# Two fused transformer blocks on one core: where the modulation pieces stand in the projection tiles, which engine copies the compressed probabilities, and when the top-k rounds run

## The chip, the cores and the metric

One NeuronCore of a Trainium2 chip runs the whole kernel. The metric is the device time of one execution in microseconds. TensorE (PE) multiplies, ScalarE (ACT) applies functions, VectorE (DVE) and GpSimd (POOL) do elementwise work and reductions, and SyncE (SP) issues the transfers (DMA) from memory into the on-chip buffers.

## The reference

Two blocks follow each other on x (1 x 512 x 1024, float32). The first is modulated by a vector c, has two attention groups and a feed-forward part; the second has two feed-forward parts with a stick-breaking attention and a recurrent group between them. The change touches only the first block up to its attention, which is, cut to what matters:

```
mod = c @ w_ada + b_ada                       # 6 x 1024 numbers: sh1, sc1, gt1, sh2, sc2, gt2
h = rms_norm(x, g_pre_mix) * (1 + sc1) + sh1
proj = h @ w_in                               # queries, keys, values, index queries and keys, gates
o_nsa = gates x (compressed + selected + window attention)     # 8 heads, 2 key groups
o_dsa = attention over the 128 keys of highest index score     # 8 heads, 1 key group
x = x + gt1 * rms_norm(concat(o_nsa, o_dsa) @ w_out, g_post_mix)
```

The compressed branch has 32 keys (one is padding), made by a small two-layer network from the rotated keys and values. The index score of a query and a key is a weighted sum of four rectified products; the top 128 of a row of up to 512 scores are found by 16 rounds of "find the 8 largest, then replace them" for each of the query tiles 1, 2 and 3 (48 rounds).

## The kernel before, in words

Activations lie with features on the 128 partitions and the 512 tokens along the free axis. Each weight tile of 128 output features is split into a high and a low part (ScalarE writes the high one, L913; VectorE the rest, L1280), and a product is three matmuls (L342 to L344). The weight tiles come in one fixed order (`STREAM`) through four ring slots.

All engines run a program written out in order, and wait on semaphores. The change lies between 58 us and 335 us of the span:

- **Projection tiles 0 to 15** (loop `for n in range(16)` on TensorE). A tile is 8 steps of k with three matmuls each, 24 matmuls. Tile 0 to 8 (`WIDE = 9`) run as a whole. ScalarE copies each finished tile (`projected`, L991), which releases `ropein`; four SP transfers swap its halves (`turn_halves`, L1882), and VectorE rotates it (`rope`).
- **The late modulation.** The last four of the six modulation vectors need 16 pieces of `w_ada` of 1 MB each (`ada_late`). They pass through two buffers: piece i goes into buffer i % 2. TensorE multiplies one with `late_piece(i)` (L404). In tiles 0 to 3 and 5 to 8 two pieces stand behind the tile's 24 matmuls; tile 4 has the step `ada_cols(1)` there (L413) instead. `logits` (L443) of the index scores follow from tile 3 on, `compress(0)` (L453) behind tile 7.
- **SP's order.** SP loads a piece with `late_load(i)` (L1856), which waits until the piece two before has been used. Pieces 2n+2 and 2n+3 (for n = 0 to 3, and one less in number for 5 to 7) stand in SP's program behind `turn_halves(n)`, which waits for `ropein` of tile n, and behind the weight tiles of `after[n]`. SP issues in order.
- **The mixed stage, tiles 9 to 15.** After every second k, TensorE runs one `pair_step(p)`, p = 0 to 27; steps 28 to 50 follow without a tile. Step p makes the scores of head pair p (L478), turns the probabilities of pair p-2 (`turn_probs`, L494) and multiplies those of pair p-3 with the values (`pv`, L510). The widths follow a pattern: query tile 3 (512 keys), 0 (128), 2 (384), 1 (256). VectorE masks the scores and takes their minimum (`masked`, L1447), ScalarE exponentiates (L1021), VectorE and POOL scale, and ScalarE copies the turned probabilities out of the bank (L1008, L1002).
- **The compressed branch** runs four times in it, at the steps of `CMP_AT`: scores at step p, softmax on VectorE at p and p+1 (`cmp_masked`, L1479; `cmp_probs`, L1492 to L1498) with one exponential on ScalarE (L1025), the turning at p+2 (`cmp_turn`, L529), the copy of the turned probabilities out of bank 4 in the same step (VectorE, L1516), and the product at p+4. `cmp_keys` prepares its 32 keys at step 4. TensorE cannot turn pair p-2 into bank 4 before this copy is done.
- **Top-k rounds** (`top_round`, L1394 and L1395) are put on VectorE at the end of tiles 5 to 8 (2 each) and then of the pair steps (one each, two in every fourth step), and end at step 31. Step 32 uses the last mask.

Of the kernel before, what the change touches and what calls it, by code (L numbers as in the profile page):

```python
# [12 lines left out]
ACT = mybir.ActivationFunctionType  # L13
# [5 lines left out]
KD = D // P  # L19
# [9 lines left out]
ROUNDS = TOPK // 8  # L29
# [107 lines left out]
def build(nc, xt, consts, cols, pos, ada, ada_late, mats, extra, out):  # L137
    ctx = ExitStack()
    with ctx:
        sems = {}  # L140

        def S(name):
            if name not in sems:
                sems[name] = ctx.enter_context(nc.semaphore(name))
            return sems[name]
# [138 lines left out]
        NP = len(pairs)  # L284
# [7 lines left out]
        steps = [(hh, c) for hh in range(HEADS) for c in (3, 2, 1, 0)]  # L292
        SLOTS = 14
        WIDE = 9
        CMP_AT = [7, 10, 18, 26]
        OUT_AT = [12, 19, 27, 35, 39, 43, 47, NP]
        slot_steps = [list(range(3 * n, min(3 * n + 3, 32))) for n in range(SLOTS)]

        NORMS = ["pre1", "post1", "f1", "post2", "g1", "mix", "g2"]
# [11 lines left out]
        def _(pe):  # L311
# [105 lines left out]
            def late_piece(i):  # L417

                q, k = i // KD, i % KD
                pe.wait_ge(S(f"ada_in{i % 4}"), 16 * (i // 4 + 3))  # L420
                if k == 0:
                    claim(7, "ada_rows", q + 2)
                ada_sums(k, ada_late_in[i % 2], range(4)).then_inc(S("ada_sums"), 1)
# [117 lines left out]
            def pair_step(p):  # L541

                if p < NP:
                    qk(p)
                if p == 0:
                    ada_cols(2)
                    compress(1)
                if p == 4:
                    cmp_keys()
                if p in CMP_AT:  # L550
                    if p == CMP_AT[0]:
                        pe.wait_ge(S("cmp_kv"), 1)
                    cmp_scores(CMP_AT.index(p))
                if p - 2 in CMP_AT:
                    cmp_turn(CMP_AT.index(p - 2))
                if p - 4 in CMP_AT:
                    cmp_out(CMP_AT.index(p - 4))
                if 2 <= p < NP + 2:
                    turn_probs(p - 2)
                if 3 <= p:  # L560
                    pv(p - 3)

            for n in range(16):
                b = n % 2 if n < WIDE else 0
                claim(b, "ropein", n + 1)
                w = take("w_in", P, "proj_full", n + 1)
                for k in range(KD):
                    mm = product(bank[:, b, :], [v[:, k, :] for v in w], [hs[:, part, k, :] for part in (0, 1)],
                                 k == 0, k == KD - 1)
                    if k == KD - 1:  # L570
                        mm.then_inc(S("proj_full"), 1)
                    if n >= WIDE and k % 2 == 1:
                        pair_step(4 * (n - WIDE) + k // 2)
                if n < 4:
                    late_piece(2 * n)
                    late_piece(2 * n + 1)
                elif n == 4:
                    ada_cols(1)
                elif n < WIDE:
                    late_piece(2 * n - 2)  # L580
                    late_piece(2 * n - 1)
                if 3 <= n < WIDE:
                    logits(2 * (n - 3))
                    logits(2 * (n - 3) + 1)
                if n == 7:
                    compress(0)
# [301 lines left out]
        def _(act):  # L888
# [120 lines left out]
                           .then_inc(S("probT"), 1)  # L1009

            def outputs(n):
                act.wait_ge(S("pv"), 9 if n == 0 else LAST_PAIR[n] + 1)
                act.activation(out_at(0, n), bank[:, 6 + (n + 1) % 2, :], ACT.Copy).then_inc(S("oT_hi"), 1)

            def pair_step(p):
                t, br, i = pairs[p]
                kv = (t + 1) * P
                for e in range(2):
                    n = 2 * (p % 2) + e
                    act.wait_ge(S("smin"), 2 * p + e + 1)  # L1020
                    act.activation(soft[p % 4][:, e, 0:kv], soft[p % 4][:, e, 0:kv], ACT.Exp, scale=-1.0,  # L1021
                                   bias=smin[:, n:n + 1], accum_out=ssum[:, n:n + 1]).then_inc(S("probs"), 1)
                if p in CMP_AT:
                    act.wait_ge(S("cmp_shift"), CMP_AT.index(p) + 1)
                    act.activation(cs[:, 1, :, :], cs[:, 0, :, :], ACT.Exp, scale=-1.0).then_inc(S("cmp_exp"), 1)  # L1025
                    own("cmp_exp")
                if p >= 2:
                    probs_turned(p - 2)
                if p == 2:
                    act.wait_ge(S("cmp_hid"), 2)  # L1030
                    act.activation(hidc[:, :, :, :].rearrange("p m g n -> p (m g n)"), bank[:, 6, 0:4 * CMP_N],
                                   ACT.Gelu_apprx_tanh).then_inc(S("cmp_gelu"), 1)
                    log_exp_tables()
                if p in OUT_AT:
                    outputs(OUT_AT.index(p))

# [217 lines left out]
        def _(dve):  # L1254
# [149 lines left out]
            for n in range(WIDE):  # L1404
                if n >= 1:
                    rope(n - 1)
                if n == 5:
                    mod_cols(1)
                ahead("w_in", n, ("w_in", 15))
                if 3 <= n:  # L1410
                    index_score(2 * (n - 3))
                    index_score(2 * (n - 3) + 1)
                while n >= 5 and rounds < 2 * (n - 4):
                    top_round(rounds)
                    rounds += 1

# [85 lines left out]
            for p in range(NP + 1):  # L1502
                if p < NP:
                    masked(p, 0)
                    masked(p, 1)
                    if p == 0:
                        late_mods()
                    if p == 4:
                        cmp_keys()
                    if p in CMP_AT:  # L1510
                        cmp_masked(CMP_AT.index(p))
                    if p - 1 in CMP_AT:
                        cmp_probs(CMP_AT.index(p - 1))
                    if p - 2 in CMP_AT:
                        dve.wait_ge(S("cmp_turned"), CMP_AT.index(p - 2) + 1)
                        dve.tensor_copy(cpt.rearrange("p a b -> p (a b)"), bank[:, 4, 0:256]).then_inc(S("cmp_probT"), 1)  # L1516
                        own("cmp_probT")
                if p >= 1:
                    scaled(p - 1)
                if p in OUT_AT[:-1]:  # L1520
                    outputs(OUT_AT.index(p))
                if p % 4 == 1 and p // 4 + WIDE < 16:
                    lo(PINDEX["w_in", min(p // 4 + WIDE + 2, 15)])
                if p == 41:
                    lo(PINDEX["w_out", 2])

                while p < NP and rounds < min(3 * ROUNDS, 2 * (WIDE - 5) + 5 * (p + 1) // 4):
                    top_round(rounds)
                    rounds += 1
            outputs(2 * NT - 1)  # L1530
# [467 lines left out]
```

## Time and profile before

| what | value |
|---|---|
| median of 3 runs | 2175.61 us (2174.71 to 2176.11) |
| profiled execution | 2178.61 us, of it 2176.8 us span |
| TensorE busy | 1993.5 us, 92% of the span |
| VectorE busy | 929.9 us, 43% |
| ScalarE busy | 701.8 us, 32% |
| GpSimd busy | 201.3 us, 9% |
| mean granted TensorE clock | 0.958 |
| read from memory | 168.36 MB, 78 GB/s over the span |

The shares are means over stages with different limits. TensorE is nearly full over most of the span; the stretch that the change touches is the one where it waits most. The time of a kernel here is the time of TensorE's program: each wait of TensorE lengthens it, and nothing behind 385 us depends on the other engines' lead in this stretch. A profile row of a timeline has the start, the time it took, and in square brackets the idle time ahead of it and what ended that.

### The profile page before, as it was taken

To read this page: it belongs to the slowest core of one execution; us is meant where nothing else is said; L and a number is where in the kernel's file an instruction comes from. 1 tells how busy PE (TensorE), PEld (TensorE's weight loads), DVE (VectorE), ACT (ScalarE), POOL (GpSimd) and SP (SyncE) were. 2 spreads that over 40 slices of the span, in tenths; PEclk is the share of its full clock that TensorE was granted. 3 is DMA by queue.
4 is the path that set the end of the run, shared out by engine and by line. 5 is a ranking of instruction groups with operands and counts; after the bars stand their busy time and mean duration, and the time that the engine had idled before them with its cause. 6 is when DMAs were issued, how large, how long until landed. Compare 5 with 4: busy or idle time off the path is not lost. (4 is left out here: it accounts for less than half of the span.)

```text
span 2176.8 us, 25083 instructions
## 1 busy us (share of the span) xinstructions
PE 1993.5 (92%) x10172; PEld 1535.8 (71%) x10172; DVE 929.9 (43%) x1534; ACT 701.8 (32%) x1139; POOL 201.3 (9%) x165
## 2 busy tenths in 40 slices
PE   5888977889999999999999889995888899999999
PEld 3555654768888876888888666653777767888887
DVE  4245776363434435332332423347434354332332
ACT  3224446242322333221222445562111143221231
POOL 0012434200000010000002003340000010000000
PEclk9898999989999999999999999997989999999999
DMA  8652100212222221232232111100000022332231
GB/s 346 236 208 72 30 25 30 78 49 97 97 96 90 96 97 52 97 113 77 97 122 72 68 68 39 39 20 0 1 1 1 1 87 78 101 112 78 97 113 52
DMA packets 44467, 176.02 MB, mean 81 GB/s; under 512 B 5568, under 2 KB 5824, under 8 KB 41024
## 3 DMA queue, kind: packets, MB, share of 16 engines
q1 hardware_dynamic: 44352, 174.41, 23.4%
q8 instruction: 81, 1.33, 0.3%
q14 instruction: 34, 0.28, 0.0%
HBM read 168.36 MB, written 2.10 MB: 78 GB/s over the span
## 5 line engine op out<-in xcount | busy, mean ns | idle before, releaser
L342 PE MATMUL bank<-hs,wsp 128*128 128x512 f32 x1368 | 550.3, 402 | 22.5 <-DVE hs L1319 11.5
L913 ACT ACTIVATE wsp<-ring 128x1024 fp32r<-128x1024 f32 (+2 forms) x244 | 268.7, 1104 | 854.7 <-PE bank L344 852.1
L343 PE MATMUL bank<-hs,wsp 128*128 128x512 f32 x1368 | 539.6, 394 | 0.0
L344 PE MATMUL bank<-hs,wsp 128*128 128x512 f32 x1368 | 538.8, 394 | 0.0
L1280 DVE TENSOR_TENSOR wsp<-ring,wsp 128x1024 fp32r<-128x1024 f32 (+2 forms) x244 | 311.9, 1281 | 410.9 <-ACT wsp L913 410.8
L342 PEld LDWEIGHTS bank<-hs,wsp 128*128 128x128 f32 x1368 | 261.2, 191 | 100.1 <-issue 38.8
L344 PEld LDWEIGHTS bank<-hs,wsp 128*128 128x128 f32 x1368 | 260.9, 191 | 56.1
L343 PEld LDWEIGHTS bank<-hs,wsp 128*128 128x128 f32 x1368 | 261.6, 191 | 54.5 <-issue 1.9
L344 PE MATMUL bank<-hids,wsp 128*128 128x512 f32 x608 | 241.0, 396 | 0.0
L343 PE MATMUL bank<-hids,wsp 128*128 128x512 f32 x608 | 241.0, 396 | 0.0
L342 PE MATMUL bank<-hids,wsp 128*128 128x512 f32 x608 | 241.0, 396 | 0.0
L1790 POOL TENSOR_TENSOR arena<-arena 128x512 f32<-128x512 f32 x24 | 43.3, 1802 | 1102.6 <-ACT arena L925 1102.6
L343 PEld LDWEIGHTS bank<-hids,wsp 128*128 128x128 f32 x608 | 114.5, 188 | 27.9
L344 PEld LDWEIGHTS bank<-hids,wsp 128*128 128x128 f32 x608 | 114.5, 188 | 27.9
L342 PEld LDWEIGHTS bank<-hids,wsp 128*128 128x128 f32 x608 | 114.5, 188 | 27.9
L1588 DVE SCALAR_TENSOR_TENSOR x<-bank,x 128x512 f32<-128x512 f32 x40 | 27.7, 691 | 173.6 <-PE bank L344 173.6
L1578 DVE TENSOR_TENSOR tmp<-tmp,bank 128x512 f32<-128x512 f32 x44 | 30.2, 687 | 128.5 <-PE bank L344 128.5
L1021 ACT ACTIVATE arena<-arena,smin 128x512 f32<-128x512 f32 (+3 forms) x96 | 53.1, 554 | 88.9 <-DVE smin L1447 88.9
L494 PE MATMUL bank<-cst,arena 128*128 128x128 f32 x240 | 41.1, 304 | 29.4 <-DVE arena L1516 11.7
L404 PE MATMUL bank<-arena,c 128*32 128x512 f32 x176 | 28.6, 751 | 38.0 <-DMA arena<-ada_late 21.6
L1225 ACT ACTIVATE wal<-bank 128x512 f32<-128x512 f32 x40 | 23.9, 597 | 116.8 <-PE bank L794 116.8
L494 PEld LDWEIGHTS bank<-cst,arena 128*128 128x128 f32 x240 | 27.7, 151 | 47.6 <-ACT tmp L1008 13.7
(290 smaller groups left out, 2198.8 us busy)
## 6 DMA issues: line engine op xcount, KB each, us to landing
ring<-m_gate SPq DMA_DIRECT2D x44, 512.0 KB, 3.3
ring<-m_up SPq DMA_DIRECT2D x44, 512.0 KB, 3.2
ring<-m_down SPq DMA_DIRECT2D x32, 704.0 KB, 4.0
ring<-m_w_in SPq DMA_DIRECT2D x38, 512.0 KB, 3.3
arena<-ada_late SPq DMA_DIRECT2D x16, 1024.0 KB, 8.0
ring<-m_w_up SPq DMA_DIRECT2D x32, 512.0 KB, 3.3
ring<-m_w_down SPq DMA_DIRECT2D x32, 512.0 KB, 3.2
ring<-m_w_out SPq DMA_DIRECT2D x16, 512.0 KB, 3.5
```

The source lines that it names most:

```text
L342: pe.matmul(out, lhs[0], rhs[0], start=start, stop=False)
L343: pe.matmul(out, lhs[0], rhs[1], start=False, stop=False)
L344: return pe.matmul(out, lhs[1], rhs[0], start=False, stop=stop)
L404: mm = pe.matmul(bank[32 * j:32 * j + 32, 7, :], c32[:, k, :], tile[:, n * T:(n + 1) * T], start=(k == 0), stop=(k == KD - 1), skip_group_ ...
L494: mm = pe.transpose(bank[:, b, (c + k) * P:(c + k + 1) * P], soft[p % 4][:, e, k * P:(k + 1) * P], const("ident"))
L913: act.activation(wsp[:, s % SPLIT, 0, 0:size], ring[:, i % RING, 0:size], ACT.Copy)\
L1021: act.activation(soft[p % 4][:, e, 0:kv], soft[p % 4][:, e, 0:kv], ACT.Exp, scale=-1.0, bias=smin[:, n:n + 1], accum_out=ssum[:, n:n + 1]) ...
L1225: act.activation(PP[:, (lv + 1) % 2, 1, :], bank[:, 6, :], ACT.Copy).then_inc(S("powerT"), 1)
L1280: dve.tensor_tensor(wsp[:, s % SPLIT, 1, 0:size], ring[:, i % RING, 0:size], wsp[:, s % SPLIT, 0, 0:size].bitcast(F32), ALU.subtract).then ...
L1578: dve.tensor_tensor(f, f, bank[:, 2 * (nn % 2) + 1, :], ALU.mult).then_inc(S("gated"), 1)
L1588: dve.scalar_tensor_tensor(out=x[:, nn, :], in0=bank[:, nn % 4, :], scalar=scale, in1=x[:, nn, :], op0=ALU.mult, op1=ALU.add).then_inc(S(" ...
L1790: pool.tensor_tensor(sq[:, 0, :], sq[:, 0, :], sq[:, k, :], ALU.add).then_inc(S("sq_sum"), 1)
```

## The change

Five edits. In tiles 0 to 3 and 5 to 8 the first of the two modulation pieces moves from the tile's end behind k = 3, the second stays at the end. `CMP_AT` becomes 9, 12, 18, 26 (it was 7, 10, 18, 26), `OUT_AT[0]` 14, and `cmp_keys` stands at step 6. The copy of the turned compressed probabilities goes from VectorE to ScalarE, there behind the two exponentials of its step. The top-k rounds are four in each of tiles 5 to 8 (16 by the end of tile 8, they were 8), and then one in every pair step up to 31.

```diff
-        CMP_AT = [7, 10, 18, 26]
-        OUT_AT = [12, 19, 27, 35, 39, 43, 47, NP]
+        CMP_AT = [9, 12, 18, 26]
+        OUT_AT = [14, 19, 27, 35, 39, 43, 47, NP]
...
-                if p == 4:
+                if p == 6:
                     cmp_keys()
...
-                if n < 4:
-                    late_piece(2 * n)
-                    late_piece(2 * n + 1)
-                elif n == 4:
-                    ada_cols(1)
-                elif n < WIDE:
-                    late_piece(2 * n - 2)
-                    late_piece(2 * n - 1)
+                    if n == 4 and k == KD - 1:
+                        ada_cols(1)
+                    elif n < WIDE and n != 4 and k in (3, KD - 1):
+                        late_piece(2 * (n - (n > 4)) + k // 4)
...
-                act.wait_ge(S("pv"), 9 if n == 0 else LAST_PAIR[n] + 1)
+                act.wait_ge(S("pv"), 11 if n == 0 else LAST_PAIR[n] + 1)
...
+                if p - 2 in CMP_AT:
+                    act.wait_ge(S("cmp_turned"), CMP_AT.index(p - 2) + 1)
+                    act.activation(cpt.rearrange("p a b -> p (a b)"), bank[:, 4, 0:256], ACT.Copy)\
+                       .then_inc(S("cmp_probT"), 1)
...
-                while n >= 5 and rounds < 2 * (n - 4):
+                while n >= 5 and rounds < 4 * (n - 4):
...
-                    if p - 2 in CMP_AT:
-                        dve.wait_ge(S("cmp_turned"), CMP_AT.index(p - 2) + 1)
-                        dve.tensor_copy(cpt.rearrange("p a b -> p (a b)"), bank[:, 4, 0:256]).then_inc(S("cmp_probT"), 1)
-                        own("cmp_probT")
...
-                while p < NP and rounds < min(3 * ROUNDS, 2 * (WIDE - 5) + 5 * (p + 1) // 4):
+                while p < NP and rounds < min(3 * ROUNDS, ROUNDS + p + 1):
```

TensorE's order before, at the end of tile 1 (`ada_in2` and `ada_in3` are the loads of pieces 2 and 3):

```order
L344 MATMUL bank<-hs,wsp 128x512
L404 MATMUL bank<-arena,c_77 32x512 [waits ada_in2]
L404 MATMUL bank<-arena,c_77 32x512 x3
L404 MATMUL bank<-arena,c_77 32x512 [waits ada_in3]
L404 MATMUL bank<-arena,c_77 32x512 x3
L342 MATMUL bank<-hs,wsp 128x512 [waits w_lo,ropein]
```

TensorE's order now, in the middle of tile 1:

```order
L344 MATMUL bank<-hs,wsp 128x512
L404 MATMUL bank<-arena,c_77 32x512 [waits ada_in2]
L404 MATMUL bank<-arena,c_77 32x512 x3
L342 MATMUL bank<-hs,wsp 128x512
L343 MATMUL bank<-hs,wsp 128x512
```

The wait for piece 2 now has twelve matmuls of the same tile in front of it and twelve behind it. SP's order between tiles 0 and 2 is the same before and after; the first transfer of each `tmp<-tmp` group waits for ScalarE's copy of the finished tile:

```order
L1882 DMA tmp<-tmp 32x512 [waits ropein]
L1882 DMA tmp<-tmp 32x512 x3
L1862 DMA ring<-m_w_in 128x1024 [waits w_lo]
L1856 DMA arena<-ada_late 128x2048 [waits ada_sums] x2
L1882 DMA tmp<-tmp 32x512 [waits ropein]
```

So the loads of pieces 2 and 3 stay behind the end of tile 0. VectorE's order before, from the second round of step 19 to step 20:

```order
L1394 MAX best_65<-arena 128x8
L1395 MATCH_REPLACE arena<-best_65,arena 128x512
L1447 ISA arena,smin<-bank,cst 128x512
L1447 ISA smin 128x1
L1447 ISA arena,smin<-bank,cst 128x512
L1447 ISA smin 128x1
L1516 COPY arena<-bank 128x256
L1457 RECIPROCAL rsum<-ssum 128x2
```

VectorE's order now at the same place (one round in step 19, no copy in step 20):

```order
L1469 TENSOR_TENSOR oalt<-bank,oalt 128x512
L1394 MAX best_65<-arena 128x8
L1395 MATCH_REPLACE arena<-best_65,arena 128x512
L1447 ISA arena,smin<-bank,cst 128x512
L1447 ISA smin 128x1
L1447 ISA arena,smin<-bank,cst 128x512
L1447 ISA smin 128x1
L1457 RECIPROCAL rsum<-ssum 128x2
```

ScalarE's order now, at the turn to a step that has the copy (L1017 are the exponentials, which wait for VectorE's minimum; L1025 is the copy):

```order
L1017 ACTIVATE arena,ssum<-arena,smin 128x256 [waits smin]
L998 ACTIVATE arena<-bank 128x2x128 [waits probs_turned,pv]
L1009 ACTIVATE oalt<-bank 128x512 [waits pv]
L1017 ACTIVATE arena,ssum<-arena,smin 128x512 [waits smin] x2
L1025 ACTIVATE arena<-bank 128x256 [waits cmp_turned]
L1004 ACTIVATE tmp<-bank 128x384 [waits probs_turned,pv]
```

The copy has moved from behind VectorE's two masks to behind ScalarE's two exponentials, which themselves follow those masks.

## Rows read from the trace of the kernel before

**Rows 1.** Busy us by engine (PE, PEld, DVE, ACT, POOL), granted clock, DMA share, GB/s
```profile
103.00:170.40 67.40, 55.87 (x279) 35.90 (x277) 26.81 (x49) 12.79 (x21) 11.52 (x9) 0.85 0.57 212
```

**Rows 2.** Timeline of TensorE, 60 to 170 us: start, time, instructions [idle before <-releaser]
```profile
63.87 1.92 PE L404 MATMUL bank<-arena,c 128*32 128x512 f32 x16
...
75.11 1.65 PE L404 MATMUL bank<-arena,c 128*32 128x512 f32 x8 [3.62 <-DMA arena<-ada_late]
79.30 1.93 PE L404 MATMUL bank<-arena,c 128*32 128x512 f32 x8 [2.53 <-DMA arena<-ada_late]
...
87.33 1.92 PE L404 MATMUL bank<-arena,c 128*32 128x512 f32 x16
...
96.78 1.07 PE L404 MATMUL bank<-arena,c 128*32 128x512 f32 x8 [1.82 <-DMA arena<-ada_late]
100.00 1.93 PE L404 MATMUL bank<-arena,c 128*32 128x512 f32 x8 [2.15 <-DMA arena<-ada_late]
...
143.96 7.36 PE L453 MATMUL bank<-arena,ring 128*128 128x64 f32 x64
...
162.79 1.93 PE L404 MATMUL bank<-arena,c 128*32 128x512 f32 x8 [5.93 <-DMA arena<-ada_late]
...
170.39 0.78 PE L342 MATMUL bank<-hs,wsp 128*128 128x512 f32 x1
```

**Rows 3.** Waits of TensorE, 60 to 520 us: us in total, times, longest
```profile
PE bank L404 <- DMA arena<-ada_late: 21.6, 8, 5.9
...
PE bank L494 <- DVE arena L1516: 11.7, 3, 5.5
```

**Rows 4.** Timeline of SP's issues behind tiles 0, 2 and 7: start, time, transfer
```profile
64.95 2.48 SPq L1882 DMA_DIRECT2D tmp<-tmp  x4
...
68.10 0.93 SPq L1856 DMA_DIRECT2D arena<-ada_late  x2
...
91.14 0.93 SPq L1856 DMA_DIRECT2D arena<-ada_late  x2
...
153.15 1.51 SPq L1856 DMA_DIRECT2D arena<-ada_late  x2
```

**Rows 5.** Timeline of TensorE in the mixed stage, steps 20, 28 and 33
```profile
279.70 1.05 PE L494 MATMUL bank<-cst,arena 128*128 128x128 f32 x6 [4.26 <-DVE arena L1516]
...
318.56 1.54 PE L494 MATMUL bank<-cst,arena 128*128 128x128 f32 x6 [5.47 <-DVE arena L1516]
...
334.08 0.48 PE L478 MATMUL bank<-arena 64*128 64x128 f32 x2 [1.61 <-DVE smin L1447]
```

**Rows 6.** Timelines of VectorE (steps 27 and 28) and of ScalarE (last row)
```profile
315.34 0.69 DVE L1394 MAX8 best<-arena 128x8 f32<-128x512 f32 x1
...
316.86 0.69 DVE L1447 CUSTOM_DVE_ANT_0 arena<-bank,cst 128x512 f32<-128x512 f32 x1
...
318.08 0.42 DVE L1516 COPY arena<-bank 128x256 f32<-128x256 f32 x1
```
```profile
318.31 0.70 ACT L1021 ACTIVATE arena<-arena,smin 128x512 f32<-128x512 f32 x1
```

**Rows 7.** Timeline of TensorE: 1st and 13th matmul of tiles 1, 2, 4; also the 8th of tile 4
```profile
65.72 0.50 PE L342 MATMUL bank<-hs,wsp 128*128 128x512 f32 x1
...
68.62 0.39 PE L342 MATMUL bank<-hs,wsp 128*128 128x512 f32 x1
...
81.16 0.80 PE L342 MATMUL bank<-hs,wsp 128*128 128x512 f32 x1
...
84.52 0.39 PE L342 MATMUL bank<-hs,wsp 128*128 128x512 f32 x1
...
103.01 0.79 PE L342 MATMUL bank<-hs,wsp 128*128 128x512 f32 x1
...
106.17 0.41 PE L343 MATMUL bank<-hs,wsp 128*128 128x512 f32 x1
...
107.33 0.39 PE L342 MATMUL bank<-hs,wsp 128*128 128x512 f32 x1
```

More of the change, by code:

```diff
@@ L1507, in _ @@
                         late_mods()
-                    if p == 4:
+                    if p == 6:
                         cmp_keys()
```

## The prediction

> **What bounds the kernel now.** I read the timeline of TensorE first, because it is busy over 92% of the span and its program is one fixed order. From 103 to 170 us it is busy for 55.9 of 67.4 us, at a granted clock of 0.85 [rows 1]. The waits there end with the landing of a modulation piece: 3.62 and 2.53 us in tile 1, 1.82 and 2.15 in tile 3, 5.93 in tile 8 [rows 2], 21.6 us in eight waits in all [rows 3]; tile 6 has a pair like tile 3's. Tile 2 has none: its two pieces run at once [rows 2], since they were issued while TensorE waited in tile 1. So one tile in two waits.
>
> SP's timeline tells why a piece is late. The load of the next two pieces stands behind the four transfers that turn the finished tile, and these begin when ScalarE has copied it: tile 0 ends at 63.9, the turning begins at 64.95, the pieces are issued at 68.10 [rows 4], 4.2 us behind the tile's end. Behind tile 2 it is 91.14 - 87.33 = 3.8. From issue to use is 75.11 - 68.10 = 7.0 us in tile 1, 96.78 - 91.14 = 5.6 in tile 3, 162.79 - 153.15 = 9.6 in tile 8 [rows 2, 4]. The second piece of a pair is there 4.2 and 3.2 us behind the first [rows 2].
>
> In the mixed stage TensorE waits for VectorE's copy of the compressed probabilities, 4.26 us at step 20 and 5.47 at step 28 [rows 5]. Such waits take 11.7 us in all [rows 3], the third is one of 2.0 us; a fourth step waits 0.3 for VectorE. The copy itself takes 0.42 us; it is late because VectorE did two top-k rounds and two masks ahead of it [rows 6].
>
> **The pieces (the large term).** The multiplication of a piece is the same work in either place, 0.96 us at the full clock (16 records in 1.92). What counts is what stands between a piece's issue and its use. Before, behind tile n: the rest of the pieces, tile n+1 whole, then the wait. Now: the second piece of tile n, half of tile n+1, then the wait, and the other half of tile n+1 behind it. SP's order is the same, and piece 2n+2 cannot be issued before tile n has ended and been copied. An earlier use of the buffer brings no earlier load. The wait begins about half a tile earlier, and the half tile behind it has lost its cover. It also now delays the end of tile n+1, with it the copy, SP's turning and the issue of the next pair. Every tile waits, where one in two did.
>
> From the end of one such tile to the end of the next is then a chain: 3.8 us to the issue, the landing, one piece, half a tile. One piece behind a wait takes 1.93 us in three rows of five, 1.65 and 1.07 in the others; I take 1.9. Half a tile takes 68.62 - 65.72 = 2.9 us without a wait, 84.52 - 81.16 = 3.4 when it follows a wait and a piece directly (tile 2), 107.33 - 103.01 = 4.3 when logits stand between (tile 4) [rows 7]. Tile 4's first seven matmuls took 106.17 - 103.01 = 3.16 us at the low clock, 0.45 each; twelve would take 5.4. I take 4.3: in tile 4 most of the slow stretch was already spent on the logits, and the waits now are longer.
>
> | end of tile | chain | at |
> |---|---|---|
> | 0 | 63.9 + one piece 0.95 | 64.9 |
> | 1 | + 4.2 + 7.0 + 1.9 + 4.3 | 82.3 |
> | 2 | + 3.8 + 6.3 + 1.9 + 4.3 | 98.6 |
> | 3 | + 3.8 + 5.6 + 1.9 + 4.3 | 114.2 |
> | 5 | + piece 0.9, logits 1.2, tile 5.6, columns and logits 1.6, tile 5.6, piece 0.9 | 130.0 |
> | 6 | + 3.8 + 6.3 + 1.9 + 4.3 | 146.3 |
> | 7 | + the same 16.3 | 162.6 |
> | 8 | + piece 0.9, logits 1.1, compress 7.2 (7.36 in its row, the end overlaps) [rows 2], then 2.0 + 9.6 + 1.9 + 4.3 | 189.6 |
> | start of tile 9 | + piece 0.9, logits 1.1 | 191.6 |
>
> The 6.3 is the mean of 7.0 and 5.6. Tile 5 doesn't wait, since its pieces are issued behind tile 3 and tile 4 stands between: issued at 118.0, landed by about 124.4, wanted at 126.2. Tile 8 costs little more than before: the loads of the compress weights hold its pieces for 9.6 us in either order, and before, the whole tile and the wait took as long. Before, tile 9 starts at 170.4 [rows 2], with about 0.5 us still to lose to the slow clock. The term is 191.6 - 170.4 - 0.5 = **+20.7 us**.
>
> Its bounds, from the rows: five chains of 3.8 + 5.6 + 1.1 + 3.4 = 13.9 us instead of 81.9 in all give 12 less, **+9**; five of 4.2 + 7.0 + 1.9 + 5.4 = 18.5 give 11 more, **+32**.
>
> The slow half tile is the term that I know least. The Trainium skill ("TensorE: Matmul & The Clock Gate", "HAM oscillation — how this bites in real kernels") describes just this loop: short stretches of matmuls between waits for loads, each of which starts at the low clock, so that the price of a change of clock is paid once per stretch. The pieces behind the waits at 79.30, 100.00 and 162.79 agree, at 1.93 us for 0.96 us of work. By that rule taken to its end every half tile runs at the low clock, which is a rival below. A second page speaks for shorter chains: by "DMA: Bandwidth & Descriptors" of the same Trainium skill ("Anatomy of one DMA — SWDGE (gpsimd) path", given for GpSimd's path), a transfer costs about 2.0 us plus its bytes at 436 GB/s, an estimate of 4.4 us for 1 MB. The five chains would be 9 us shorter by it. No load of a piece landed that soon in this trace, and other loads stand ahead of each in the queue, so I stay with the rows.
>
> **More top-k rounds in tiles 5 to 8.** Eight more rounds of about 0.98 us (256 wide) on VectorE, four per tile instead of two. They lie in tiles where TensorE waits for loads; tiles 6, 7 and 8 leave VectorE over 8 us idle each. Behind tile 8 VectorE has then 3.9 us of rounds ahead of the first mask instead of 2; TensorE meanwhile runs the logits, the first scores and 7.3 us of compress, and asks for that mask's bank only at the second pair. Cost nothing; without that cover 2 us.
>
> **Fewer rounds in the mixed stage.** Steps 19, 27 and 31 lose one 512-wide round each, 316.86 - 315.34 = 1.5 us [rows 6], just where VectorE is last.
>
> **The copy on ScalarE.** VectorE copied at 318.08, right behind its second mask. ScalarE has the same mask to wait for, then the second exponential (it began at 318.31 and took 0.70) and the reading of its sum, 0.19: it could begin at 319.2, 1.1 us later, for a copy of equal length. That is +1.1 at each of the four places while TensorE waits there. With the lost round: step 20, -1.6 + 1.1 = -0.5; step 28, -1.5 + 1.1 = -0.4. The first two now lie at steps 11 and 14. Step 11 had at its old place 0.3 us of wait, and VectorE does two masks, the compressed softmax (1.8), a weight tile (1.2) and two rounds in the steps ahead: I take +1.0. Step 14 likewise has one round less but a weight tile more: +0.4.
>
> **The other shifts.** `cmp_keys` at step 6 waits for the same 10 small copies on VectorE as at step 4 (a wait of 2.25 us before): 0. The compressed scores at step 9 and 12 wait less for VectorE than at 7 and 10 (0.53 and 1.62 us before), -1.0. At step 33 the wait of 1.61 us for the mask [rows 5] goes, since step 31 has one round less: -1.5; ScalarE's copies are late next there.
>
> **The sum.** Mixed stage: 1.0 + 0.4 - 0.5 - 0.4 - 1.0 - 1.5 = -2.0, between -6 (the copy's lateness hidden, and less slow clock behind each wait) and +4 (the copy late in full at all four, no gain from the rounds). Total +20.7 - 2.0 = **+18.7 us**. The profiled execution of 2178.6 would become 2197.3; the median of the runs is 3.0 below the profiled one, so 2175.6 + 18.7 = **2194.3 us**.
>
> **Rivals.**
> - *Half clock throughout.* TensorE is idle some 6 us in each 16 and never gets its clock back within a half tile: chains of 18.5 us, +32 - 2 = +30, 2205.6. For it: 1.93 us for a piece behind each longer wait. Against: tile 2 was back at full pace within three microseconds of its wait [rows 7].
> - *VectorE was the real limit (faster).* If the mixed stage's waits are all VectorE's lateness, the 8 rounds and four copies taken off it remove the 11.7 us of waits for L1516, 1.6 at step 33, and about 6 us of slow clock behind them: -19. With the projection at its low bound, +9, it ends 10 us faster, 2165.6. It decides from the point at which ScalarE's copy is done when TensorE has turned the compressed probabilities; [rows 6] speak against it, since the masks and exponentials ahead alone take over 2 us.
> - *The change doesn't do what it says to the waits.* SP could have the pieces loaded ahead of the turning, and the earlier use of a buffer would count. Then the 21.6 us of waits for pieces [rows 3] would go, -20, 2155. The issues behind the turning [rows 4] and SP's order nearly exclude it.
> - *Small sum.* Chains at the low bound and the mixed stage at its best, with ends near +4: 2179.6. It needs every term at its low end.
>
> **How the numbers follow.** Forecast 0.75; half clock 0.13; small sum 0.06, half of it within 0.2% (4.4 us, about what a measurement of this kernel can tell from no change) and half above; VectorE the limit 0.04; earlier loads 0.02. Slower 0.91, same 0.03, faster 0.06. The range goes from +7 (the term's low bound less 2) to +30, 2182 to 2206.
>
> **What the profile after would show.** In each of tiles 1, 2, 3, 6, 7 and 8 one wait of 5 to 9 us for `ada_late` behind the 12th matmul, none or little at the tile's end, none in tile 5; SP's issues of pieces 3.8 us behind each tile's end; tile 9 starting near 191. In the mixed stage waits of about 3.8 and 5.1 us at steps 20 and 28, now for ScalarE. It would be wrong if the tiles follow each other at less than 14 us, which a landing in 5 us or a clock that stays high would do, or if the mixed stage is shorter by more than 6 us.

## The result and the profile after

The changed kernel takes 2191.9 us (median of 6 runs, 2182.1 to 2198.8) against 2175.4 us before (6 runs). The ratio is 1.0075, 95% interval 1.0056 to 1.0093: slower by 16.3 us, between 12 and 20. Forecast were 18.7 us and 2194.3 us. The profiled execution took 2185.3 us (span 2183.5) and lies in the faster half of its runs; its granted clock, told below, goes with that.

The piece waits moved into the tiles and grew. This is TensorE's timeline after, the rows of the pieces alone, to set beside [rows 2]. The pieces without a bracket stand at a tile's end and find their data there:

```profile
66.39 1.07 PE L404 MATMUL bank<-arena,c 128*32 128x512 f32 x8
76.57 1.94 PE L404 MATMUL bank<-arena,c 128*32 128x512 f32 x8 [6.16 <-DMA arena<-ada_late]
82.46 1.07 PE L404 MATMUL bank<-arena,c 128*32 128x512 f32 x8
91.89 1.94 PE L404 MATMUL bank<-arena,c 128*32 128x512 f32 x8 [5.40 <-DMA arena<-ada_late]
98.57 1.07 PE L404 MATMUL bank<-arena,c 128*32 128x512 f32 x8
108.11 1.93 PE L404 MATMUL bank<-arena,c 128*32 128x512 f32 x8 [5.48 <-DMA arena<-ada_late]
113.61 1.07 PE L404 MATMUL bank<-arena,c 128*32 128x512 f32 x8
...
128.41 1.90 PE L404 MATMUL bank<-arena,c 128*32 128x512 f32 x8 [3.03 <-DVE mod L1290]
133.96 1.06 PE L404 MATMUL bank<-arena,c 128*32 128x512 f32 x8
...
143.88 1.93 PE L404 MATMUL bank<-arena,c 128*32 128x512 f32 x8 [5.06 <-DMA arena<-ada_late]
150.20 1.07 PE L404 MATMUL bank<-arena,c 128*32 128x512 f32 x8
...
159.64 1.94 PE L404 MATMUL bank<-arena,c 128*32 128x512 f32 x8 [4.59 <-DMA arena<-ada_late]
164.97 1.07 PE L404 MATMUL bank<-arena,c 128*32 128x512 f32 x8
...
185.76 1.94 PE L404 MATMUL bank<-arena,c 128*32 128x512 f32 x8 [8.55 <-DMA arena<-ada_late]
191.66 1.06 PE L404 MATMUL bank<-arena,c 128*32 128x512 f32 x8
```

There is one wait in the middle of every tile that has pieces, none at its end, and each piece behind a wait takes nearly twice the time of the one without (1.94 and 1.07 us).

SP's timeline after, to set beside [rows 4], has the issue 3.8 us behind the tile's end (86.27 - 82.46, and 102.39 - 98.57), as before:

```profile
83.19 2.41 SPq L1878 DMA_DIRECT2D tmp<-tmp  x4
85.64 0.58 SPq L1858 DMA_DIRECT2D ring<-m_w_in  x1
86.27 0.93 SPq L1852 DMA_DIRECT2D arena<-ada_late  x2
...
102.39 0.93 SPq L1852 DMA_DIRECT2D arena<-ada_late  x2
```

TensorE's largest waits from 60 to 520 us after, to set beside [rows 3]:

```profile
PE bank L404 <- DMA arena<-ada_late: 35.2, 6, 8.6
PE bank L494 <- ACT arena L1025: 10.7, 3, 4.8
```

The waits for pieces grew from 21.6 to 35.2 us; those for the compressed copy are 10.7 where they were 11.7, and end now with ScalarE's copy (L1025). At step 20 and 28, to set beside [rows 5]:

```profile
295.23 1.08 PE L494 MATMUL bank<-cst,arena 128*128 128x128 f32 x6 [3.50 <-ACT arena L1025]
...
333.18 1.54 PE L494 MATMUL bank<-cst,arena 128*128 128x128 f32 x6 [4.82 <-ACT arena L1025]
```

For all kernels below, three marks divide the span: the first score product (step 0, L478), the first product with `w_out`, and the end. Between the first two lies the mixed stage. "Idle" is what TensorE's busy time leaves of it, so it holds all its waits, and "clock" is the mean granted TensorE clock in it. All numbers are of the profiled execution.

| kernel | step 0 at | w_out at | mixed stage | idle in it | clock in it | rest | span |
|---|---|---|---|---|---|---|---|
| before | 172.3 | 385.4 | 213.1 | 34.9 | 0.93 | 1791.4 | 2176.8 |
| after | 195.3 | 395.2 | 199.9 | 29.6 | 0.97 | 1788.3 | 2183.5 |
| pieces only (e1) | 198.0 | 406.9 | 208.9 | 34.9 | 0.95 | 1788.9 | 2195.8 |
| all but pieces (e2) | 172.2 | 379.5 | 207.3 | 29.6 | 0.93 | 1793.5 | 2173.0 |
| loads first (e3) | 157.4 | 363.3 | 205.9 | 30.7 | 0.94 | 1788.7 | 2152.0 |
| piece behind k = 5 (e4) | 181.4 | 390.3 | 208.9 | 29.6 | 0.93 | 1787.9 | 2178.2 |
| pieces at end, loads first (e5) | 153.7 | 363.5 | 209.8 | 30.0 | 0.92 | 1790.0 | 2153.5 |
| copy only (e6) | 173.6 | 387.3 | 213.7 | 37.0 | 0.93 | 1788.9 | 2176.2 |
| rounds only (e7) | 176.1 | 382.5 | 206.4 | 29.4 | 0.93 | 1786.2 | 2168.7 |
| shift only (e8) | 174.8 | 382.2 | 207.4 | 34.1 | 0.95 | 1788.4 | 2170.6 |
| columns early (e14) | 190.5 | 401.0 | 210.5 | 28.1 | 0.90 | 1790.3 | 2191.3 |
| loads first, columns early (e11) | 153.5 | 360.9 | 207.4 | 30.7 | 0.93 | 1789.2 | 2150.1 |
| the same, copy on VectorE (e13) | 151.4 | 360.4 | 209.0 | 25.5 | 0.90 | 1793.2 | 2153.6 |
| the same, ScalarE's copy first (e12) | 152.3 | 347.3 | 195.0 | 24.2 | 0.97 | 1792.2 | 2139.5 |

### The profile page after: what moved, and what is told of

The parts are those of the page before. It is cut to its first block and busy times, and to the rows that moved or that the text cites. A ratio compares the mean times of both kernels' runs of the same rounds, so it can differ in the third digit from the quotient of the medians.

```text
span 2183.5 us, 25083 instructions
## 1 busy us (share of the span) xinstructions
PE 1989.3 (91%) x10172; PEld 1531.6 (70%) x10172; DVE 930.1 (43%) x1530; ACT 702.8 (32%) x1143; POOL 202.5 (9%) x165
## 5 line engine op out<-in xcount | busy, mean ns | idle before, releaser
L344 PEld LDWEIGHTS bank<-hids,wsp 128*128 128x128 f32 x608 | 114.6, 189 | 27.8
L404 PE MATMUL bank<-arena,c 128*32 128x512 f32 x176 | 31.7, 810 | 53.1 <-DMA arena<-ada_late 35.2
L1017 ACT ACTIVATE arena<-arena,smin 128x512 f32<-128x512 f32 (+3 forms) x96 | 53.1, 554 | 73.0 <-DVE smin L1447 73.0
L494 PE MATMUL bank<-cst,arena 128*128 128x128 f32 x240 | 38.8, 293 | 25.7 <-ACT arena L1025 10.7
```

Source lines behind the costliest of these rows:

```text
L344: return pe.matmul(out, lhs[1], rhs[0], start=False, stop=stop)
L404: mm = pe.matmul(bank[32 * j:32 * j + 32, 7, :], c32[:, k, :], tile[:, n * T:(n + 1) * T], start=(k == 0), stop=(k == KD - 1), skip_group_ ...
L494: mm = pe.transpose(bank[:, b, (c + k) * P:(c + k + 1) * P], soft[p % 4][:, e, k * P:(k + 1) * P], const("ident"))
```

## The experiments

Each time below is the median of 4 to 12 runs, and each ratio is against runs of the kernel before that were made beside them.

**Which edit costs: the pieces alone, and all without the pieces.** The first takes only this edit into the kernel before:

```diff
+                    if n == 4 and k == KD - 1:
+                        ada_cols(1)
+                    elif n < WIDE and n != 4 and k in (3, KD - 1):
+                        late_piece(2 * (n - (n > 4)) + k // 4)
```

> The kernel before with one of the five edits: the first modulation piece of a tile behind k = 3. Theory 1 (the chain tile end, copy, turning, issue, landing, piece, half a tile): all of the loss is here, tile 9 starts 21 to 24 us later than before, +18 to +24 us in all, about 2196. Theory 2 (the loss comes from the copy on ScalarE or from VectorE's longer list of rounds in the tiles, the pieces only move the same wait from the end of a tile into its middle): within 8 us of before.

Measured: 2200.2 us, ratio 1.0106 (1.0087 to 1.0124), +23 us. Step 0 is 25.7 us later than before and tile 9 starts 26.0 us later, more than the 21 to 24 expected; its wait in tile 8 was 10.6 us. The second is the changed kernel with this edit undone.

> The changed kernel with its modulation pieces back at the end of the tiles; the other four edits stay. Theory 1: faster than before, by 2 us if the prediction's small terms hold, by 6 to 13 if the shorter mixed stage seen in the profile of the changed kernel (201.5 us against 215.0) is due to these edits; 2162 to 2173. Theory 2: 8 us or more slower than before.

Measured: 2170.3 us, ratio 0.9978 (0.9965 to 0.9990), -4.8 us, between the 2 and the 6 to 13 that were named; step 0 comes at 172.2, as before. So the pieces cost some 23 us and the other four edits gain some 5; the sum of 18 agrees with the measured 16 inside the intervals. Theory 2 has fallen.

**Where in the tile the cut lies.**

```diff
-                    elif n < WIDE and n != 4 and k in (3, KD - 1):
-                        late_piece(2 * (n - (n > 4)) + k // 4)
+                    elif n < WIDE and n != 4 and k in (5, KD - 1):
+                        late_piece(2 * (n - (n > 4)) + (k == KD - 1))
```

> The changed kernel with the first piece of each tile behind k = 5 instead of k = 3, so that six matmuls stand behind its wait instead of twelve. Theory 1 (what stands behind the wait is on the chain): each of six chains is 1.4 to 2 us shorter, 8 to 12 us faster than the changed kernel, about 2181. Rival (splitting a tile costs, wherever the cut is): within 3 us of the changed kernel.

Measured: 2183.5 us, ratio 1.0026 (1.0015 to 1.0037), +5.7 us against before, 8.4 us faster than the changed kernel by the medians and 10.7 by the ratios; step 0 is 13.9 us earlier. The wait in tile 1 is 4.12 us, and only six matmuls follow it:

```profile
74.70 1.94 PE L404 MATMUL bank<-arena,c 128*32 128x512 f32 x8 [4.12 <-DMA arena<-ada_late]
79.43 1.06 PE L404 MATMUL bank<-arena,c 128*32 128x512 f32 x8
88.81 1.16 PE L404 MATMUL bank<-arena,c 128*32 128x512 f32 x8 [3.99 <-DMA arena<-ada_late]
92.76 1.19 PE L404 MATMUL bank<-arena,c 128*32 128x512 f32 x8
```

Tiles 1 and 2 end 13.3 us apart (92.76 - 79.43), where it was 16.1 in the changed kernel (98.57 - 82.46). Part of this is the work that left the chain, and part is the clock: the second tile's piece took 1.16 us and not 1.94, which is 0.8 of the 2.8 us by itself. The price depends on how much stands behind the wait, and the rival, a price of the cut itself, has fallen.

**SP's order.**

```diff
+                if n in pieces:
+                    late_load(pieces[n])
                 if n != VC:
                     turn_halves(n)
+                if n in pieces:
+                    late_load(pieces[n] + 1)
                 while n in after and i <= place[after[n]]:
                     tile_load(i)
                     i += 1
-                if n in pieces:
-                    late_load(pieces[n])
-                    late_load(pieces[n] + 1)
```

> The changed kernel with SP's order changed: the load for a tile's first piece is issued ahead of the turning of the finished tile (as soon as the buffer is free, in the middle of the tile), the second right behind the turning, the weight tiles after them. Theory 1: the chain is cut, a piece is issued about 7 us earlier, the wait in the middle of tiles 1 to 3 and 6 to 8 shrinks from 5 to 9 us to under 2, tile 9 starts at 165 or earlier; 25 to 35 us faster than the changed kernel, 2157 to 2167. Rival (the transfers' bandwidth is the limit, two pieces and a weight tile per projection tile): the waits stay near their size, less than 8 us gained.

Measured: 2153.0 us, ratio 0.9893 (0.9875 to 0.9911), 23 us faster than before and about 39 faster than the changed kernel; step 0 is 37.9 us earlier. SP's timeline and TensorE's waits from 60 to 200 us show how:

```profile
77.86 0.33 SPq L1852 DMA_DIRECT2D arena<-ada_late  x1
82.71 2.41 SPq L1878 DMA_DIRECT2D tmp<-tmp  x4
```
```profile
PE bank L404 <- DMA arena<-ada_late: 6.9, 4, 5.6
PE bank L404 <- DVE mod L1290: 3.5, 1, 3.5
```

The load is issued in the middle of tile 1, 4.9 us ahead of the turning, and of the 35.2 us of waits 6.9 are left. One of 5.6 stays in tile 1, whose piece was issued behind two weight tiles. That piece was issued at 66.11 and used at 75.86, so an issue 4.8 us earlier than in the changed kernel brought it 0.7 us earlier: there what stands ahead of it in the queue decided, and not its own issue. Everywhere else the rival of bandwidth has fallen, and tile 8's wait of 8.55 went too, since its piece no longer queues behind the three tiles of compress weights. The gain is larger than the 25 to 35 us expected, which is about what the waits alone could give. From the start of tile 0 to step 0 the stage is 37.8 us shorter: TensorE idles 27.8 us less in it, and is busy for 9.9 us less with the same work, at a granted clock of 0.95 instead of 0.84.

> Pieces at the end of the tiles as before, the other four edits as in the changed kernel, and the same new order on SP (first piece's load ahead of the turning, second right behind it, weight tiles last). The first load cannot be issued before the tile's end here, 3 us earlier than before instead of 7. Theory 1: 6 to 12 us faster than the kernel without the order change, and slower than or level with the version that has a piece in mid-tile. Rival (bandwidth): less than 3 us gained.

Measured for the pieces at the tiles' end with the new order: 2155.3 us, ratio 0.9899 (0.9879 to 0.9919), 15 us faster than with the old order and more than the 6 to 12 expected. The reason is the same: up to step 0 it is 19.1 us shorter, 9.7 of them idle time and 9.4 busy time, at a clock of 0.96 instead of 0.85. It cannot be told apart from the version with a piece in mid-tile. So the early release of a buffer, which is what a piece in mid-tile can bring, is worth nothing measurable even where SP can use it: issuing the loads ahead of the other transfers is what pays.

**The other edits one by one,** each put alone into the kernel before. The copy:

> The kernel before with the copy of the compressed probabilities on ScalarE, behind the two exponentials of its step, and nothing else. By the prediction's step (the copy comes 1.1 us later at each of four places, 0.42 us less on VectorE): +2 to +4 us against before, TensorE's waits for the copy 14 to 16 us in all instead of 11.7. Rival (VectorE is the limit of the mixed stage and its relief pays for the later copy): level or faster.

Measured: 2177.9 us, ratio 1.0011 (0.9998 to 1.0023), +2.4 us, as expected, though the interval reaches from -0.4 to +5 us and so does not exclude that nothing changed. The waits for it, from 160 to 400 us:

```profile
PE bank L494 <- ACT arena L1029: 14.4, 3, 6.3
```

These are 2.87, 5.16 and 6.34 us where they were 2.00, 4.26 and 5.47: 0.9 us more each. The rounds:

> The kernel before with the new placing of the top-k rounds only: 16 by the end of tile 8, then one in each step. By the prediction's steps: 1.5 us each gained at steps 20, 28 and 33 and up to 1 at step 12, -4 to -6 us, about 2169 to 2171. Rival (the rounds in tiles 5 to 8 delay VectorE's other work there, the weight split or the first masks): level or slower.

Measured: 2169.5 us, ratio 0.9964 (0.9952 to 0.9976), -7.8 us where -4 to -6 was expected (the interval is -5 to -10). The same waits, from 160 to 400 us:

```profile
PE bank L494 <- DVE arena L1516: 8.0, 3, 3.9
```

They are 1.46, 2.63 and 3.95 us, shorter by 0.5, 1.6 and 1.5, and the one at step 33 is gone: 5.3 us of waits in all, as expected. The shift of the compressed steps:

> The kernel before with the compressed steps at 9 and 12 and its keys at step 6 only. By the prediction: within 2 us of before (a little less wait at the scores, as much at the keys). Rival (the shift is what shortens the mixed stage, since the first two copies no longer meet VectorE's late phase): -3 us or more.

Measured: 2171.2 us, ratio 0.9979 (0.9966 to 0.9991), -4.6 us. The prediction's step did not expect this, and the rival of that run (-3 or more) held. Its waits explain only about 1 us (11.4 us for the copy where it was 11.7 and the 0.3 of step 9; 3.9 for the scores where it was 3.7; 1.9 for the keys where it was 2.2). The mixed stage is 5.7 us shorter in its trace: 0.8 us less idle time and 4.9 us less busy time, at a clock of 0.95 against 0.93. Why the shift gains this stays open. The three alone add to -10, together they give -4.8. Each of the four numbers has an interval of some 2.7 us to either side, so whether their gains add is not shown.

**The wait in tile 5.** In it the first piece of the second group of modulation rows waits for VectorE (L1290, which frees bank 7), an event that the prediction did not have.

```diff
-                if n == 5:
+                if n == 4:
                     mod_cols(1)
                 ahead("w_in", n, ("w_in", 15))
```

> The changed kernel with VectorE taking in the second group of modulation columns at the end of tile 4, ahead of the weight split, instead of behind the index scores. It sizes the wait in tile 5 that the prediction did not have: the wait of 3.0 us goes and the slow clock behind it, 3 to 5 us faster than the changed kernel. Rival (the following chain begins as late anyway): no difference.

Measured: 2194.4 us, ratio 1.0082 (1.0069 to 1.0094): no difference from the changed kernel, where 3 to 5 us were expected. The rival came out, but not for its reason: in the trace the wait is gone, what follows does begin earlier, and step 0 comes 4.8 us earlier, at 190.5. Then the mixed stage takes 210.5 us at a clock of 0.90, where the changed kernel's profiled execution took 199.9 at 0.97. TensorE's row for this stage (the changed kernel's first, then this one's):

```profile
195.30:395.20 199.90, 170.33 (x1304) 0.97 0.13 40
```
```profile
190.50:401.00 210.50, 182.49 (x1303) 0.90 0.12 38
```

> The changed kernel with SP's loads first (as in the earlier run of that order) and VectorE's step that takes in the second group of modulation columns one tile earlier in its program, ahead of the weight split. It is to show whether TensorE's wait in tile 5 (3.0 us in the changed kernel, 3.5 with the loads first) is VectorE's queue: then it vanishes and the kernel is 3 to 5 us faster than with loads first alone, 2148 to 2150. Rival (it is the piece that is late there, the semaphore of VectorE only came last by a little): a wait for the load of 2 to 3 us takes its place, less than 1 us gained.

Measured with the loads first: 2149.6 us, ratio 0.9880 (0.9866 to 0.9894), 3 us faster than with the loads first alone in the medians, though the intervals overlap, so that the gain itself is not shown. No wait stands in tile 5, neither for VectorE nor for a load, so it was VectorE's queue.

**The copy's place.** Two kernels go on from the last one. In one the copy goes back to VectorE, in the other ScalarE does it ahead of the exponentials:

```diff
+                if p - 2 in CMP_AT:
+                    act.wait_ge(S("cmp_turned"), CMP_AT.index(p - 2) + 1)
+                    act.activation(cpt.rearrange("p a b -> p (a b)"), bank[:, 4, 0:256], ACT.Copy)\
+                       .then_inc(S("cmp_probT"), 1)
                 for e in range(2):
                     n = 2 * (p % 2) + e
                     act.wait_ge(S("smin"), 2 * p + e + 1)
...
-                if p - 2 in CMP_AT:
-                    act.wait_ge(S("cmp_turned"), CMP_AT.index(p - 2) + 1)
-                    act.activation(cpt.rearrange("p a b -> p (a b)"), bank[:, 4, 0:256], ACT.Copy)\
-                       .then_inc(S("cmp_probT"), 1)
```

> Loads first and columns early, with the copy back on VectorE (behind its masks, as in the kernel before). From the run of the copy alone: 0.9 us less wait at each of three places, 2 to 3 us faster than with the copy behind ScalarE's exponentials, about 2147; slower than the version with ScalarE's copy ahead of them if that one works.

Measured for VectorE's copy: 2152.5 us, ratio 0.9884 (0.9867 to 0.9900), where 2 to 3 us faster was expected; it can't be told apart from the kernel with ScalarE's copy (0.9880). Its waits are shorter as expected (8.2 us where they were 10.7, and 5.1 us less idle time in the stage), and its mixed stage is not, 209.0 us at a clock of 0.90.

> Loads first and columns early as in the last run, and ScalarE's copy of the compressed probabilities ahead of the two exponentials of its step instead of behind them. If the copy waits only because it stands behind VectorE's masks, TensorE's 10.7 us of waits for it fall under 3 and the kernel is 4 to 8 us faster than with the copy behind, about 2143. Rival (the wait only moves, since TensorE then comes sooner to the scores that VectorE has not masked): less than 2 us gained, and waits for the minimum of VectorE in their place.

Measured for ScalarE's copy ahead of the exponentials: 2143.7 us, ratio 0.9853 (0.9839 to 0.9867), 32 us faster than before, 5.9 us faster than with the copy behind them (4 to 8 expected), and the fastest kernel of the study. TensorE's waits in it, from 145 to 400 us, and the row of its mixed stage:

```profile
PE bank L494 <- ACT arena L1016: 1.4, 3, 0.5
```
```profile
152.28:347.28 195.00, 170.80 (x1304) 0.97 0.13 41
```

The wait for the copy fell from 10.7 to 1.4 us and nothing took its place but 0.9 us for a mask at step 33 and 2 us more for ScalarE's other copies. The stage is 12.4 us shorter in the two traces, 6.5 of it idle time; the other 5.9 are busy time at a clock of 0.97 instead of 0.93, which the same program can have or lack (see below). The copy is an operation whose input is ready and for which TensorE waits; behind two exponentials that wait for VectorE it stood in the wrong place.

## Why the prediction was right

**The chain of a tile: right as a mechanism, with the ends helped by luck.** The forecast's ends of tiles against the second pieces' starts in the profile after:

| end of tile | forecast | measured |
|---|---|---|
| 1 | 82.3 | 82.5 |
| 2 | 98.6 | 98.6 |
| 3 | 114.2 | 113.6 |
| 5 | 130.0 | 134.0 |
| 6 | 146.3 | 150.2 |
| 7 | 162.6 | 165.0 |
| 8 | 189.6 | 191.7 |

The ends agree better than the terms do. Tile 0 ended at 66.4 where 64.9 was taken, 1.3 us of it because the work ahead of the tiles ended later in this execution. The five chains of tiles 1 to 3, 6 and 7 took 78.2 us in all (16.1, 16.1, 15.0, 16.2 and 14.8) where 81.9 were taken, and tile 5 had a wait of 3.0 us that the forecast had not.

The issue came 3.8 us behind the tile, as taken (4.5 behind tile 0, where 4.2 were). The landing took 5.7, 5.6, 5.7, 6.1 and 5.6 us where 7.0, 6.3, 5.6, 6.3 and 6.3 were taken, which is most of the difference, and 9.6 in tile 8, as taken. The half tile behind the wait took 4.0, 4.7, 3.6, 4.4 and 3.4 us (from a piece's end to the next start) where 4.3 were taken, the piece 1.9 as taken. The clock of the half tile was neither high nor low throughout (2 to 9 of its twelve matmuls took 0.59 us or more, the others about 0.4), so the rival of half clock was wrong by its size. The waits of 5.1 to 8.6 us lie in the range named, except 4.59 in tile 7. From the start of tile 0 to step 0 the changed kernel takes 135.7 us instead of 114.0, +21.7, and the run of this edit alone gives +23 us, where +20.7 stood.

**Tile 5: a wait that the step missed.** "Tile 5 doesn't wait" looked only at the loads. The first piece of a group of eight also claims bank 7, which VectorE frees when it takes in the columns of the group before. The piece at mid-tile claims it half a tile earlier, and VectorE's weight split and index scores stand ahead of it. It cost 3.0 us and the slow clock behind them. The version with the columns early is 4.2 us shorter from tile 0 to step 0, but not in the time. That its cost in the whole kernel is nil is not shown: the two kernels' mixed stages differ by more, with less idle time in the slower one (28.1 us against 29.6).

**The extra rounds in the tiles: free, as said.** The groups of four rounds begin at 138.2, 155.3, 169.4 and 197.2 us in the profile after. The first three ended before the weight split of the next tile was due, the fourth lies under TensorE's compress work, and no wait of TensorE follows from it. In the kernel with all but the pieces the tiles took 114.1 us up to step 0, as before (114.0).

**The mixed stage: right in sign, less than half in size.** Forecast -2.0, measured -4.8 with the pieces undone (the interval is -2 to -8). TensorE's idle time in the stage fell from 34.9 to 29.6 us, so the waits alone gave -5.2. Against the terms of the forecast:

- The copies stood at +0.5 and gave -1.0. The two lost rounds took 1.6 and 1.5 us from the waits at steps 20 and 28, as said; the later copy cost 0.9 us each and not 1.1; the waits after were forecast at 3.8 and 5.1 us and are 3.50 and 4.82. At step 14 it is 2.42 us, as forecast (2.0 + 0.4). The +1.0 at step 11 was wrong: TensorE doesn't wait for the copy there.
- The waits for the scores are 0.52, 1.02 and twice 0.75, in all 3.0 us where they were 3.7, a gain of 0.7 where 1.0 stood.
- The wait at step 33 went, 1.6 us where 1.5 stood.
- Some 2 us of small waits went that the forecast had no term for. The largest is one of 1.20 us for ScalarE's copy L1002 at 364 us. Kernels with the same program in this stage have it (e3, e11) or lack it (after, e2), so it is no sure gain of the edits.

The bound of -6 held.

**What the forecast gave no place to.** The profiled execution after has a mixed stage of 199.9 us, 13.2 shorter than before. Idle time is 5.3 of that; the other 7.9 are busy time. The kernels after, e2, e3, e4, e11 and e14 have the same program in this stage and nearly the same waits (10.7 or 10.8 us for the copy, 28.1 to 30.7 us of idle time in all), and it takes them 199.9, 207.3, 205.9, 208.9, 207.4 and 210.5 us, at clocks of 0.97, 0.93, 0.94, 0.93, 0.93 and 0.90. After and e2 idle for 29.6 us both, and their 7.4 us of difference are busy time. What differs is the granted clock. Over the whole span it goes with the time of the changed kernel's runs too: 0.962 at 2182.1 and 2185.3 us, 0.959 at 2192.3, 0.955 at 2198.8. So the profiled execution at 2185.3 was a fortunate one, and the forecast met the median (2194.3 against 2191.9) better than the profile (2197.3 against 2185.3). That the median came so close is in part luck: the pieces cost 1 to 2 us more than forecast and the mixed stage gained 3 us more, and the two errors have opposite signs. What sets the clock's pattern in a given execution stays open.

The rival with VectorE as the real limit gave -19 for the mixed stage and was wrong. Taking work off VectorE was worth about the waits that it removed (5.2 us of idle time and 4.8 us of time in e2, 5.3 and 7.8 in e7); that it was worth more is not shown, since e7's interval is -5 to -10.

## What to carry to other kernels

- A wait for a load belongs where the load's issue is far behind it in time. Before moving a use earlier, look at what stands ahead of the load in the queue that issues it: if the issue hangs on the end of the same tile, an earlier use only puts more work behind the wait, and it delays the next issue too. Moving the load ahead of other transfers in SP's program gained 15 us with the uses at the tiles' ends and 39 with one in mid-tile, where moving the use cost 23.
- When an operation moves to another engine, ask what stands ahead of it there. The same copy cost 0.9 us more of wait each time behind two exponentials, and took 9 us of waits away ahead of them.
- A gain of a few microseconds in waits can vanish in the granted clock. The kernels with six or more runs spread by 10 to 17 us here, so such steps are read from their waits and judged by the medians of many runs.

## What the runs showed of the hardware

VectorE and GpSimd slow each other down. In the changed kernel GpSimd's four additions (L1802) run from 119.96 to 126.16 us, and VectorE's weight split falls into them; the same instruction took 1.23 us just ahead:

```profile
119.96 6.20 POOL L1802 TENSOR_TENSOR arena<-arena,col 64x496 f32<-64x496 f32 x4 [67.57 <-DVE arena L1368]
```
```profile
115.51 1.23 DVE L1280 TENSOR_TENSOR wsp<-ring,wsp 128x1024 fp32r<-128x1024 f32 x1 [10.88 <-ACT wsp L909]
...
122.83 2.21 DVE L1280 TENSOR_TENSOR wsp<-ring,wsp 128x1024 fp32r<-128x1024 f32 x1 [3.02 <-ACT wsp L909]
124.97 2.10 DVE L1383 SCALAR_TENSOR_TENSOR arena<-tmp,widx,arena 128x256 f32<-128x256 f32 x2
```

The split took 1.0 us longer and the two index scores about 1.0 together (0.48 for one alone, just ahead). These 2 us stand directly ahead of the step that TensorE waits for in tile 5; without them its wait of 3.0 us would be about 1.0, an estimate from these rows. GpSimd's four additions took 6.20 us, where they took 5.35 with VectorE idle in the kernel before. Which of the two pays differs: in the kernel with the loads first and the columns early (e11) the split ran beside them in 1.23 us, the two index scores took 2.94, and the four additions 6.34. The Trainium skill, "SBUF — State Buffer", section "Who interferes with whom", says that an instruction of VectorE with two inputs in the on-chip buffer contends with one of GpSimd that reads it, and that the order of issue decides who is blocked. The split, the index scores and the additions are of that kind, and the trace agrees that they contend; whether one is blocked or both are slowed can't be read from the sums.

The other thing not expected is the spread of the clock over executions of one program, told above.
